# Latent attention's first eight heads: values times probabilities as three products of rounded operands in two column halves, in place of a plain fp32 product

## The chip, the cores and the metric

The kernel runs on one core of one Trainium2 chip. The metric is the device time of one execution in microseconds, median over repeated runs. Times are in us throughout.

## What is computed

The program is a stack of six layers over 512 tokens of width 1024: four mixers (convolution, forgetting attention, gated delta rule, sliding-window attention), a bidirectional linear recurrence with MLP, and multi-head latent attention with MLP. Only the latent attention changes in substance. Cut to what matters:

```python
MLA_HEADS, MLA_NOPE, MLA_ROPE, MLA_V = 16, 128, 64, 128
q = (rms_norm_2(cq, q_norm) @ w_uq).reshape(b, s, 16, 192)
k_nope, v = per head, rms_norm_2(ckv, kv_norm) @ w_ukv        # 128 + 128 columns a head
scores = (q_nope @ k_nope.T + rope(q_rope) @ rope(k_rope).T) * (128 + 64) ** -0.5
probs = softmax(scores)                                      # all 512 keys, no mask
o = probs @ v                                                # 512 x 128 a head
out = concat(o over the 16 heads) @ w_o
```

## The kernel before

**Numbers in two parts.** Nearly every product is done as three: each fp32 operand x is held as a rounded part ("high", type fp32r) and the rest ("low" = x minus high, also fp32r), and TensorE adds high times high, low times high and high times low in one PSUM bank. ScalarE makes the high part with a copy, then VectorE (or GpSimd, for the weights, line 374) the low part with a subtraction. The product of values and probabilities is an exception in this kernel: line 3339 multiplies plain fp32 tiles.

**Jobs.** Weights come as 388 jobs of 512 KB through four slots. SyncE loads them (line 284), ScalarE rounds them (line 358), GpSimd makes the low part (line 374), TensorE uses them, and each job of a slot owns one of the PSUM banks 0 to 3.

**Attention by pairs.** The sixteen heads are done as eight pairs, four in part 0 and four in part 1; each part is a loop of two trips with two pairs, followed by eight output jobs (`out_pe`). A pair begins with its projections: queries (n1 and the job's bank), keys (k0, k1) and values (v23 in an auxiliary bank, v01 in the job's bank). Then come, for head h (0 or 1) and the block of 128 queries q (0 to 3), the steps

- `s{h}{q}`: scores of 128 queries by 512 keys, five products (lines 3324 to 3328). VectorE takes the maximum (line 3505), ScalarE the exponential with its sum (line 3415) into `b.p[h][q % 2]`.
- `t{h}{q}`: VectorE divides by the sum (lines 3509 and 3510), TensorE transposes the four 128x128 blocks into a bank (line 3333), ScalarE copies them out into `b.pt[h]` (line 3419).
- `o{h}`: values times transposed probabilities into one bank (line 3339), 384 columns and then 128. ScalarE rounds the result (line 3423), VectorE makes its low part (line 3515).

**What orders the work.** The order on each engine is written out by hand: `MLA_ORDER` for TensorE, `MLA_SCALAR_ORDER` for ScalarE, `MLA_VECTOR_ORDER` for VectorE. Each engine does its list strictly in order. The steps share four auxiliary PSUM banks (4 to 7) in the ring `mla_aux`: use number u takes bank u modulo 4, and TensorE may begin a use (`ring.claim`) only when the last reader of the use four places before it has freed the bank (`ring.read`). So t02 takes the bank of s03, s13 that of s12, t12 that of t01, t03 that of t11 and o0 that of t02.

**Statistics.** The three stages `hg_post`, `ple0_post` and `mla_post` sum squares over partitions with a matmul by a matrix of ones, and `keep_busy` (line 477) fills TensorE's waits there with products whose result nobody reads: one between the sums and four behind them, 15 in all.

Of the kernel before, what the change touches and what calls it, by code (L numbers as in the profile page):

```python
# [38 lines left out]
def const_layout():  # L39

    i = np.arange(P)
    c = {}
    c["ident"] = np.eye(P)
    c["ones"] = np.ones((P, S))
    c["eps"] = np.full((P, 1), EPS)
    c["eps_squared"] = np.full((P, 1), EPS * EPS)
    c["ident2"] = np.tile(np.eye(CH), (2, 1))
    m = np.zeros((P, 2 * H8))
    for h in range(H8):
        m[[h, 32 + h], h] = 1.0  # L50
# [160 lines left out]
def hybrid_stack(nc, weights, x_t, p_t, consts, masks, params, positions, positions_2, sinks, out):  # L211
# [9 lines left out]
    with ctx:  # L221
        def sb(name, shape, dt=F32):
            return ctx.enter_context(nc.sbuf_tensor(name, shape, dt))
# [22 lines left out]
        K.w_hi = sb("weights_high", [P, SLOTS, D], F32R)  # L246
        K.w_lo = sb("weights_low", [P, SLOTS, D], F32R)
        K.X = sb("residual", [P, DT, S])
        K.M = sb("mixed", [P, DT, S])
        K.act_hi = sb("activations_high", [P, 2 * DT, S], F32R)  # L250
        K.act_lo = sb("activations_low", [P, 2 * DT, S], F32R)
        K.ident_r = sb("ident_r", [P, P], F32R)
        K.mask_r = sb("mask_r", [P, 2 * P], F32R)
        K.sel_r = sb("select_rows", [P, 2, P], F32R)
        K.sq = sb("squares", [P, 2, S])
        K.rstd, K.rstd_r = both("rstd", [P, S])
        K.root, K.root_r = both("root", [P, S])
        K.y, K.y_r = both("to_split", [P, 2, S])
        K.work = sb("work", [P, WORK])
        K.ps = [ctx.enter_context(nc.psum_tensor(f"bank{k}", [P, S], F32)) for k in range(8)]  # L260
        K.job_sems = dict(raw=[sem(f"raw_full{k}") for k in range(SLOTS)], high=sem("weights_high_ready"),
                          low=sem("weights_low_ready"), done=sem("jobs_done"),
# [131 lines left out]
def bank_of(e, c):  # L394
    return e.K.ps[c % SLOTS]
# [81 lines left out]
def keep_busy(e, n):  # L477

    K = e.K
    for _ in range(n):  # L480
        K.nc.tensor.matmul(K.ps[IDLE_BANK][:, :], K.c("ident"), K.c("ones"), start=True, stop=True)


LATE_SQUARES = 2
# [455 lines left out]
def conv_dve(e):  # L940
# [19 lines left out]
    e.eng.sem_inc(K.sem("x_ready"), DT)  # L960
    e.eng.sem_inc(K.sem("y_done"), DT)
    e.eng.wait_ge(K.sem("constants_in"), 16)
    e.steps.step(v.tensor_copy(K.ident_r[:, :], K.c("ident")))
    wf = K.param[:, K.cols["final_norm_w"]:K.cols["final_norm_w"] + DT]
    w = K.param[:, K.cols["pre_mix_norm_2"]:K.cols["pre_mix_norm_2"] + DT]
    e.steps.step(v.tensor_tensor(K.hg_cols[:, 0:DT], wf, w, ALU.mult))
# [1 line left out]
    e.steps.wait()  # L968
    e.steps.step(v.tensor_scalar(K.hg_cols[:, DT:2 * DT], K.hg_cols[:, DT:2 * DT], EPS, None, ALU.add))
    e.eng.wait_ge(K.sem("masks_in"), 16)  # L970
    v.tensor_copy(K.mask_r[:, :], K.M[:, 0, 0:2 * P]).then_inc(K.sem("masks_ready"), 1)
    e.steps.step(v.memset(b.u[:, 0:2], 0.0))
    take(renorm_vector(e, "conv", c0), 2 * DT)
    e.steps.wait()
# [201 lines left out]
def fox_dve(e):  # L1176
# [20 lines left out]
    st.wait()  # L1197
    st.step(v.tensor_tensor(x, ee, x, ALU.subtract))
    st.wait()
    st.step(v.tensor_tensor_scan(ncum, K.c("ones")[0:H8, :], x, 0.0, ALU.mult, ALU.add))  # L1200
    take(renorm, DT)
    st.wait()
    st.step(v.tensor_copy(b.rows[0:H8, :], ncum))
# [1968 lines left out]
def mla_written():  # L3172
# [12 lines left out]
MLA_SCALAR_ORDER = ["s00", "s10", "s01", "s11", "t00", "t10", "s02", "s12", "t01", "s03",  # L3185
                    "t11", "t02", "s13", "t12", "t03", "o0", "t13", "o1"]

MLA_VECTOR_ORDER = ["k0", "k1", "s00", "s10", "t00", "s01", "s11", "t10", "t01", "s02", "t11", "s12", "s03",
                    "t02", "t12", "t03", "s13", "t13", "o0", "o1"]


def mla_buffers(K):
    b = Names()
    (qr, v_tok, p, pt0, pt1) = carve(K, (DT, S), (QT, 2 * P), (2, S), (QT, S), (QT, S))
    mx, sums, rec = K.sinks[:, 0:4], K.sinks[:, 4:8], K.sinks[:, 8:12]

# [12 lines left out]
    return b
# [12 lines left out]
def mla_pe(e):  # L3222
# [50 lines left out]
    for part, out in ((0, "mla_outa"), (1, "mla_outb")):  # L3273
        c0 = FIRST_JOB[("mla_a", "mla_b")[part]]
        with e.eng.Fori(0, 2) as i:
            for s in range(2):
                trip, c = i + 2 * part, c0 + 2 * s
                mla_pair_pe(e, b, ring, ident, trip, c, i, s)
        out_pe(e, out, "mla_y", A_TILES, part * DT)
    stat_tensor(e, "mla_post")  # L3280

# [12 lines left out]
    return ins  # L3294


def mla_pair_pe(e, b, ring, ident, trip, c, i, s):

    K, nc, mm = e.K, e.K.nc, e.K.nc.tensor.matmul
    job_start(e, c, i)  # L3300
# [13 lines left out]
    for what in MLA_ORDER[4:]:  # L3314
        use, h, q = f"{what}_{s}", int(what.strip("stov")[0]), int(what[-1])
        ring.claim(use, trip)
        dst = ring.bank(use)
        if what[0] == "s":
            if q == 0:
                ring.wait_read(f"k{h}_{s}", trip)  # L3320
                ring.wait_read(f"n1_{s}", trip)
            settle(e)
            cut = slice(q * P, (q + 1) * P)
            mm(dst[:, :], b.qn_hi[:, h, cut], b.kn_hi[:, h, :], start=True, stop=False)  # L3324
            mm(dst[:, :], b.qn_lo[:, h, cut], b.kn_hi[:, h, :], start=False, stop=False)  # L3325
            mm(dst[:, :], b.qn_hi[:, h, cut], b.kn_lo[:, h, :], start=False, stop=False)
            mm(dst[:, :], b.qs[h][:, cut], b.kr_hi[:, :], start=False, stop=False)  # L3327
            ins = mm(dst[:, :], b.qs[h][:, cut], b.kr_lo, start=False, stop=True)  # L3328
        elif what[0] == "t":
            e.eng.wait_ge(K.sem(f"mla_p{h}"), trip * 8 + s * 4 + q + 1)  # L3330
            settle(e)
            for t in range(QT):
                ins = nc.tensor.transpose(dst[:, t * P:(t + 1) * P], b.p[h][q % 2][:, t * P:(t + 1) * P], ident)  # L3333
        else:
            for last, cut in ((2, slice(0, 3 * P)), (3, slice(3 * P, S))):
                ring.wait_read(f"t{h}{last}_{s}", trip)
                settle(e)
                for t in range(QT):
                    ins = mm(dst[:, cut], b.v_tok[:, t, h * P:(h + 1) * P], b.pt[h][:, t, cut],  # L3339
                             start=t == 0, stop=t == QT - 1)  # L3340
        ring.written(ins)


def mla_act(e):
# [41 lines left out]
    for part, out in ((0, "mla_outa"), (1, "mla_outb")):  # L3386
        c0 = FIRST_JOB[("mla_a", "mla_b")[part]]
        with e.eng.Fori(0, 2) as i:
            for s in range(2):
# [13 lines left out]
                weight_high(e, c + 1 + AHEAD, i)  # L3403
                use = f"v23_{s}"
                ring.wait(use, trip)
                ring.read(use, act(mla_flat(b.v_tok, 2), ring.bank(use)[:, :], ACT.Copy))
                job_wait(e, c + 1, i)
                act(mla_flat(b.v_tok, 0), bank_of(e, c + 1)[:, :], ACT.Copy).then_inc(K.job_sems["bank"][(c + 1) % SLOTS], 1)
                for what in MLA_SCALAR_ORDER:
                    use, h, q = f"{what}_{s}", int(what[1]), int(what[-1])  # L3410
                    if what[0] == "s":
                        e.eng.wait_ge(K.sem(f"mla_max{h}"), trip * 8 + s * 4 + q + 1)
# [3 lines left out]
                                           accum_out=b.stat(b.sum, h, q)))  # L3416
                    elif what[0] == "t":
                        ring.wait(use, trip)
                        ring.read(use, act(b.pt[h][:, :, q * P:(q + 1) * P],
                                           ring.bank(use)[:, :].rearrange("p (a d) -> p a d", d=P), ACT.Copy))  # L3420
                    else:
                        ring.wait(use, trip)
                        act(at(K.act_hi, i * 4 + 2 * s + h), ring.bank(use)[:, :], ACT.Copy) \
# [8 lines left out]
def mla_dve(e):  # L3432
# [43 lines left out]
    for part, out in ((0, "mla_outa"), (1, "mla_outb")):  # L3476
        c0 = FIRST_JOB[("mla_a", "mla_b")[part]]
        with e.eng.Fori(0, 2) as i:
            st.enter(i, 2 * MLA_STEPS)
            for s in range(2):  # L3480
                trip, c = i + 2 * part, c0 + 2 * s
                high = K.sem("mla_high")
# [9 lines left out]
                    e.eng.wait_ge(high, trip * 12 + s * 6 + 3 + h)  # L3492
                    step(v.tensor_tensor(b.qs[h][other, :], turned[own, :], b.qs[h][own, :].bitcast(F32), ALU.subtract))
                e.eng.sem_inc(K.sem("mla_staged"), 1)
                for what in MLA_VECTOR_ORDER:
                    use, h, q = f"{what}_{s}", int(what.strip("stovk")[0]), int(what[-1])
                    if what[0] == "k":
                        ring.wait(use, trip)
                        e.eng.wait_ge(high, trip * 12 + s * 6 + 5 + h)
                        ring.read(use, v.tensor_tensor(b.kn_lo[:, h, :], ring.bank(use)[:, :],  # L3500
# [174 lines left out]
```

## Time and profile before

| what | value |
|---|---|
| median of 3 runs | 2720.49 (2719.74 to 2721.52) |
| the profiled execution, its own time | 2723.37 |
| its span | 2721.6 |
| granted TensorE clock, mean | 0.996 |
| busy: TensorE, VectorE, ScalarE, GpSimd | 2666.7, 1394.2, 1231.0, 1076.5 |

A row of the timeline gives the start, the duration, the engine, the line of the program, the operation with its output and inputs, how many records were merged, and in brackets how long the engine had been idle and who ended that. The durations of TensorE's records overlap, since matmuls are pipelined; the distance from one start to the next is what a matmul costs in a stream. One plain fp32 matmul leaves two records. The projections and the steps of one attention pair repeat almost to the nanosecond from pair to pair.

### The profile page before, as it was taken

The page shows a single profiled execution, that of the slowest core. Times are in us where ns is not written, and L with a number is a line of the kernel's source. Part 1 is how long each engine was busy: PE and PEld are TensorE (multiplying, and loading weights), DVE is VectorE, ACT ScalarE, POOL GpSimd, SP SyncE. Part 2 cuts the span into 40 slices and gives each one's busy share as a digit, 9 for nine tenths or more (in the row PEclk, how much of TensorE's full clock was granted, in tenths as well). Part 3 has the DMA queues.
Part 4 walks back from the last instruction along what each step waited for, and adds up shares of the span by engine and source line. Part 5 has one row for each costly group of instructions (what it writes and reads, how often), then busy time and mean ns, then how long its engine had stood idle before and what let it go on. Part 6 is the DMA issues. An engine that isn't in the chain of part 4 may idle for free.

```text
span 2721.6 us, 41980 instructions
## 1 busy us (share of the span) xinstructions
PE 2666.7 (98%) x13878; PEld 2135.9 (78%) x13878; DVE 1394.2 (51%) x2452; ACT 1231.0 (45%) x1916; POOL 1076.5 (40%) x803
## 2 busy tenths in 40 slices
PE   7999999989999999999999999999999999999999
PEld 6887777767777777788887888887778887888886
DVE  7335333677778567787755321128753454221126
ACT  5324433555554455565544433235554463333234
POOL 5554333324233333443434544444412213544442
PEclk9999999999999999999999999999999999999999
DMA  4332222211121222222222333332211212333331
GB/s 159 102 99 85 77 76 71 70 55 56 37 62 47 68 70 63 85 78 67 72 70 85 101 98 95 92 112 85 78 39 46 62 31 70 101 100 92 95 106 55
DMA packets 59643, 211.89 MB, mean 78 GB/s; under 512 B 6688, under 2 KB 7072, under 8 KB 59552
## 3 DMA queue, kind: packets, MB, share of 16 engines
q1 hardware_dynamic: 57744, 206.89, 25.5%
q10 hardware_dynamic: 1520, 2.75, 0.3%
q8 instruction: 56, 0.92, 0.1%
q0 software_dynamic: 288, 1.05, 0.1%
q14 instruction: 35, 0.29, 0.0%
HBM read 208.57 MB, written 2.10 MB: 77 GB/s over the span
## 4 chain that ended last, share of the span: by engine, by line
PE 69%; DVE 5%; issue 2%; ACT 2%; POOL 0%; DVEq 0%; ACTq 0%; POOLq 0%
PE bank L1327 18%; PE bank L1329 17%; PE bank L1328 17%; PE bank L3339 2%; PE bank L1455 2%; PE bank L3333 1%; PE bank L424 1%; DVE activations_low L454 1%; PE bank L426 1%; PE bank L425 1%; PE bank L1480 1%; PE bank L3324 1%; PE bank L2191 1%; PE bank L3327 1%; PE bank L3325 1%
## 5 line engine op out<-in xcount | busy, mean ns | idle before, releaser
L374 POOL TENSOR_TENSOR weights_low<-weights_raw,weights_high 128x512 fp32r<-128x512 f32 x776 | 1047.3, 1373 | 1450.0 <-ACT weights_high L358 1425.4
L1327 PE MATMUL bank<-activations_high,weights_high 128*128 128x512 f32 x2912 | 1179.1, 405 | 29.6 <-POOL weights_low L374 13.1
L1329 PE MATMUL bank<-activations_high,weights_low 128*128 128x512 f32 x2912 | 1140.1, 392 | 0.0
L1328 PE MATMUL bank<-activations_low,weights_high 128*128 128x512 f32 x2912 | 1139.2, 391 | 0.0
L1327 PEld LDWEIGHTS bank<-activations_high,weights_high 128*128 128x128 f32 x2912 | 549.4, 189 | 164.5 <-issue 18.6
L1329 PEld LDWEIGHTS bank<-activations_high,weights_low 128*128 128x128 f32 x2912 | 548.7, 188 | 116.4
L1328 PEld LDWEIGHTS bank<-activations_low,weights_high 128*128 128x128 f32 x2912 | 550.0, 189 | 108.6 <-issue 6.7
L358 ACT ACTIVATE weights_high<-weights_raw 128x1024 fp32r<-128x1024 f32 x384 | 404.0, 1053 | 282.1 <-PE bank L1329 275.2
L2972 DVE TENSOR_TENSOR mixed<-bank,mixed 128x512 f32 (+1 forms) x48 | 33.2, 692 | 193.9 <-PE bank L1329 193.9
L2916 ACT ACTIVATE to_split<-work 128x512 f32<-128x512 f32 x64 | 40.5, 632 | 181.5 <-DVE work L2958 181.5
L2958 DVE SCALAR_TENSOR_TENSOR work<-bank,rstd 128x512 f32<-128x512 f32 x64 | 44.2, 690 | 140.2 <-PE bank L1329 134.1
L2963 DVE TENSOR_TENSOR activations_low<-to_split,activations_high 128x512 f32 x64 | 46.6, 728 | 104.6 <-ACT activations_high L2918 104.6
L1455 PEld LDWEIGHTS bank<-work 64*64 64x64 f32 x1344 | 47.4, 134 | 30.5 <-issue 30.5
L1036 ACT ACTIVATE activations_high<-to_split 128x512 fp32r<-128x512 f32 (+1 forms) x24 | 15.2, 632 | 103.3 <-DVE to_split L2370 48.1
L3505 DVE TENSOR_REDUCE sink_rows<-bank 128x1 f32<-128x512 f32 x64 | 44.1, 689 | 30.0 <-PE bank L3328 28.7
L1455 PE MATMUL bank<-work 64*64 64x64 f32 x1344 | 58.3, 223 | 1.0 <-DVE work L1966 0.9
L3339 PE MATMUL bank<-work 128*128 128x384 f32 (+1 forms) x256 | 58.8, 383 | 0.0
L1775 POOL TENSOR_TENSOR mixed<-mixed 128x512 f32<-128x512 f32 x7 | 9.6, 1376 | 120.6 <-ACT mixed L1694 120.6
L424 PE MATMUL bank<-activations_high,weights_high 128*128 128x512 f32 x136 | 56.5, 416 | 0.2 <-DVE activations_low L454 0.2
L1842 DVE SCALAR_TENSOR_TENSOR work<-work 128x512 f32<-128x512 f32 x66 | 54.6, 827 | 2.0 <-DVE mixed L1981 0.2
L792 DVE TENSOR_TENSOR root<-root,squares 128x512 f32<-128x512 f32 x44 | 40.1, 912 | 29.9 <-ACT squares L783 29.4
L783 ACT ACTIVATE squares<-residual 128x512 f32<-128x512 f32 x32 | 20.2, 632 | 76.9 <-DVEq L808 76.9
(473 smaller groups left out, 3334.7 us busy)
## 6 DMA issues: line engine op xcount, KB each, us to landing
weights_raw<-weights SPq DMA_DIRECT2D x388, 512.0 KB, 3.6
out_t<-residual SPq DMA_DIRECT2D x8, 256.0 KB, 2.1
residual<-x_t ACTq DMA_DIRECT2D x2, 512.0 KB, 7.5
residual<-x_t POOLq DMA_DIRECT2D x2, 512.0 KB, 9.9
work<-p_t ACTq DMA_DIRECT2D x2, 512.0 KB, 4.6
const<-consts SPq DMA_DIRECT2D x1, 713.0 KB, 12.7
const<-consts SPq DMA_DIRECT2D x1, 321.0 KB, 11.6
root<-positions ACTq DMA_DIRECT2D x1, 256.0 KB, 3.1
```

Of the source, the lines that this page charges most:

```text
L358: e.K.nc.scalar.activation(e.K.w_hi[:, s, :], e.K.raw[:, s, :], ACT.Copy).then_inc(js["high"], 1)
L374: K.nc.gpsimd.tensor_tensor(K.w_lo[:, s, part], K.raw[:, s, part], K.w_hi[:, s, part].bitcast(F32), ALU.subtract).then_inc(K.job_sems["low ...
L424: K.nc.tensor.matmul(dst, wh, K.act_hi[:, t, :], start=first, stop=False)
L1327: K.nc.tensor.matmul(dst, wh, K.act_hi[:, t, :], start=k == 0, stop=False)
L1328: K.nc.tensor.matmul(dst, wh, K.act_lo[:, t, :], start=False, stop=False)
L1329: ins = K.nc.tensor.matmul(dst, wl, K.act_hi[:, t, :], start=False, stop=k == len(tiles) - 1)
L1455: ins = mm(chunk(bank(use)[h, :], c), lhs[h, c, :], rhs[h, c, :], start=True, stop=True)
L1842: ins = v.scalar_tensor_tensor(t, u[:, n:n + S], b.taps[:, 4 * part + n:4 * part + n + 1], t, ALU.mult, ALU.add)
L2958: v.scalar_tensor_tensor(relu, bank_of(e, c0 + r)[:, :], 0.0, K.rstd[:, :], ALU.max, ALU.mult) \
L2963: v.tensor_tensor(at(K.act_lo, n + DT), K.y[:, 0, :], at(K.act_hi, n + DT).bitcast(F32), ALU.subtract).then_inc(K.sem("split_done"), 1)
L3339: ins = mm(dst[:, cut], b.v_tok[:, t, h * P:(h + 1) * P], b.pt[h][:, t, cut], start=t == 0, stop=t == QT - 1)
L3505: v.tensor_reduce(mx, ring.bank(use)[:, :], AX.X, ALU.max, negate=True).then_inc(K.sem(f"mla_max{h}"), 1)
```

## The change

In part 0 (the first eight heads) the product of values and probabilities is done in three products of rounded operands, in two halves of 256 columns. For that ScalarE's copies of the values and of the transposed probabilities now write rounded tiles (`b.v_hi`, `b.pt_hi`), and VectorE subtracts them from the same PSUM banks to make `b.v_lo` (steps v0, v1 in its list) and `b.pt_lo` (steps l00 to l13). The banks of v23, v01 and of every t step are freed by VectorE's subtraction and no longer by ScalarE's copy. VectorE's list becomes `MLA_SPLIT_ORDER`; ScalarE's differs from before only in that t03 stands ahead of t12. Part 1 stays as it was.

Beside that, the constant matrix of ones shrinks from 512 to 128 columns, `ident_r` goes, and the small rounded tables share a tensor with `b.v_lo`. With it the filling matmuls of `keep_busy` have 384 columns instead of 512, and a cumulative sum in the forgetting attention (line 1200) reads its ones from a single broadcast column.

```diff
-    c["ones"] = np.ones((P, S))
+    c["ones"] = np.ones((P, P))
...
-        K.M = sb("mixed", [P, DT, S])
+        K.M, K.M_r = both("mixed", [P, DT, S])
...
-        K.ident_r = sb("ident_r", [P, P], F32R)
-        K.mask_r = sb("mask_r", [P, 2 * P], F32R)
-        K.sel_r = sb("select_rows", [P, 2, P], F32R)
+        K.rows_r = sb("rows_rounded", [P, 2 * QT, P], F32R)
+        K.mask_r = K.rows_r[:, 0:2, :].rearrange("p a b -> p (a b)")
+        K.sel_r = K.rows_r[:, 2:4, :]
...
     for _ in range(n):
-        K.nc.tensor.matmul(K.ps[IDLE_BANK][:, :], K.c("ident"), K.c("ones"), start=True, stop=True)
+        K.nc.tensor.matmul(K.ps[IDLE_BANK][:, 0:3 * P], K.c("ident"), K.const[:, 0:3 * P], start=True, stop=True)
...
-    e.steps.step(v.tensor_copy(K.ident_r[:, :], K.c("ident")))
...
-    st.step(v.tensor_tensor_scan(ncum, K.c("ones")[0:H8, :], x, 0.0, ALU.mult, ALU.add))
+    st.step(v.tensor_tensor_scan(ncum, K.c("ones")[0:H8, 0:1].broadcast_to([H8, S]), x, 0.0, ALU.mult, ALU.add))
...
+MLA_SPLIT_SCALAR = ["s00", "s10", "s01", "s11", "t00", "t10", "s02", "s12", "t01", "s03",
+                    "t11", "t02", "s13", "t03", "t12", "o0", "t13", "o1"]
+
+MLA_COPIES = [use for use in MLA_SPLIT_SCALAR if use[0] == "t"]
+
+MLA_SPLIT_ORDER = ["k0", "k1", "v0", "v1", "s00", "s10", "t00", "s01", "s11", "t10", "t01", "l00", "s02", "t11", "l10", "s12",
+                   "l01", "s03", "t02", "t12", "l11", "t03", "s13", "l02", "t13", "l03", "l12", "o0", "l13", "o1"]
...
+        elif halves:
+            own = slice(h * P, (h + 1) * P)
+            ring.wait_read(f"v23_{s}", trip)
+            evacuated(e, c + 1, i)
+            for last, cut in ((1, slice(0, 2 * P)), (3, slice(2 * P, S))):
+                ring.wait_read(f"t{h}{last}_{s}", trip)
+                settle(e)
+                for t in range(QT):
+                    mm(dst[:, cut], b.v_hi[:, t, own], b.pt_hi[h][:, t, cut], start=t == 0, stop=False)
+                    mm(dst[:, cut], b.v_hi[:, t, own], b.pt_lo[h][:, t, cut], start=False, stop=False)
+                    ins = mm(dst[:, cut], b.v_lo[:, t, own], b.pt_hi[h][:, t, cut], start=False, stop=t == QT - 1)
...
+                if part == 0:
+                    act(mla_flat(b.v_hi, 2), ring.bank(use)[:, :], ACT.Copy).then_inc(K.sem("mla_rounded"), 1)
+                    job_wait(e, c + 1, i)
+                    act(mla_flat(b.v_hi, 0), bank_of(e, c + 1)[:, :], ACT.Copy).then_inc(K.sem("mla_rounded"), 1)
...
+                        if part == 0:
+                            act(b.pt_hi[h][:, :, q * P:(q + 1) * P], src, ACT.Copy).then_inc(K.sem("mla_rounded"), 1)
...
+                    if what[0] == "v":
+                        e.eng.wait_ge(K.sem("mla_rounded"), trip * 20 + s * 10 + 1 + h)
+                        bank = bank_of(e, c + 1) if h else ring.bank(f"v23_{s}")
+                        step(v.tensor_tensor(mla_flat(b.v_lo, 2 - 2 * h), bank[:, :], mla_flat(b.v_hi, 2 - 2 * h).bitcast(F32),
+                                             ALU.subtract))
...
+                    elif what[0] == "l":
+                        use, cut = f"t{what[1:]}_{s}", slice(q * P, (q + 1) * P)
+                        e.eng.wait_ge(K.sem("mla_rounded"), trip * 20 + s * 10 + 2 + MLA_COPIES.index(f"t{what[1:]}") + 1)
+                        ring.read(use, v.tensor_tensor(b.pt_lo[h][:, :, cut], ring.bank(use)[:, :].rearrange("p (a d) -> p a d", d=P),
+                                                       b.pt_hi[h][:, :, cut].bitcast(F32), ALU.subtract))
```

On VectorE, in the middle of a pair of part 0, from the maximum of s02 to that of s03. Before (3505 is the maximum, 3509 and 3510 the division; `squares` and `work` hold the two heads' probabilities):

```order
L3505 TENSOR_REDUCE sink_rows<-bank 128x1
L3509 RECIPROCAL sink_rows<-sink_rows 128x1
L195 REGISTER_ALU
L3510 TENSOR_SCALAR squares<-squares,sink_rows 128x512
L1290 REGISTER_ALU
L3505 TENSOR_REDUCE sink_rows<-bank 128x1
L1290 REGISTER_ALU
L3505 TENSOR_REDUCE sink_rows<-bank 128x1
```

The same place after the change (3549 is the maximum, 3553 and 3554 the division, 3539 the new subtraction):

```order
L3549 TENSOR_REDUCE sink_rows<-bank 128x1
L3553 RECIPROCAL sink_rows<-sink_rows 128x1
L195 REGISTER_ALU
L3554 TENSOR_SCALAR squares<-squares,sink_rows 128x512
L3538 REGISTER_ALU
L3539 TENSOR_TENSOR mixed_rounded<-bank,work_rounded 128x4x128
L1289 REGISTER_ALU
L3549 TENSOR_REDUCE sink_rows<-bank 128x1
L3538 REGISTER_ALU
L3539 TENSOR_TENSOR mixed_rounded<-bank,work_rounded 128x4x128
L1289 REGISTER_ALU
L3549 TENSOR_REDUCE sink_rows<-bank 128x1
```

Between the maxima of s02 and s12 the subtraction l10 has come in, and between those of s12 and s03 the subtraction l01; another, l00, stands right ahead of the first row.

On TensorE, the end of a pair of part 0. Before (3333 is a transpose, 3339 the product of values and probabilities):

```order
L3333 MATMUL bank<-const,work 128x128 x4
L1283 REGISTER_ALU
L3339 MATMUL bank<-work 128x384 x4
L3339 MATMUL bank<-work 128x128 x4
L3333 MATMUL bank<-const,squares 128x128 x4
```

After the change (3344 is the transpose; the three lines 3353 to 3355 come eight times for a head, four for each half of the columns):

```order
L3344 MATMUL bank<-const,work 128x128 x4
L1282 REGISTER_ALU
L3353 MATMUL bank<-work_rounded 128x256
L3354 MATMUL bank<-mixed_rounded,work_rounded 128x256
L3355 MATMUL bank<-work_rounded,rows_rounded 128x256
```

Eight plain fp32 matmuls of a head have become 24 rounded ones of 256 columns; the transposes around them stand where they stood.

## Rows read from the trace of the kernel before

**Rows 1.** The page: the span, and busy time of each engine

```profile
span 2721.6 us, 41980 instructions
PE 2666.7 (98%) x13878; PEld 2135.9 (78%) x13878; DVE 1394.2 (51%) x2452; ACT 1231.0 (45%) x1916; POOL 1076.5 (40%) x803
```

**Rows 2.** Busy time of each engine over the second pair of part 0

```profile
1995.52:2025.27 29.75, 29.75 (x162) 24.05 (x160) 15.23 (x32) 17.98 (x36) 5.10 (x4) 1.00 0.12 36
```

**Rows 3.** Timeline, TensorE: projections of values, then the second pair's end

```profile
2002.45 0.28 PE L3291 MATMUL bank<-weights_high,activations_high 128*128 128x256 f32 x1
...
2005.20 0.28 PE L3293 MATMUL bank<-weights_low,activations_high 128*128 128x256 f32 x1
...
2016.49 0.63 PE L3333 MATMUL bank<-const,work 128*128 128x128 f32 x4
2016.95 0.60 PE L3333 MATMUL bank<-const,squares 128*128 128x128 f32 x4
2017.39 0.60 PE L3333 MATMUL bank<-const,work 128*128 128x128 f32 x4
2017.89 3.71 PE L3339 MATMUL bank<-work 128*128 128x384 f32 x16
2021.44 0.60 PE L3333 MATMUL bank<-const,squares 128*128 128x128 f32 x4
2021.88 3.64 PE L3339 MATMUL bank<-work 128*128 128x384 f32 x16
2025.27 0.47 PE L424 MATMUL bank<-activations_high,weights_high 128*128 128x512 f32 x1
```

**Rows 4.** Timeline, VectorE: two subtractions from a bank, one after the other

```profile
1973.14 1.29 DVE L3500 TENSOR_TENSOR activations_low<-bank,const_rounded 128x512 fp32r<-128x512 f32 x2 [0.33 <-DVE activations_high L3493]
```

**Rows 5.** Timeline, VectorE and ScalarE in the middle of the second pair

```profile
2011.56 0.49 DVE L3510 TENSOR_SCALAR work<-work,sink_rows 128x512 f32<-128x512 f32 x1
2011.57 1.25 ACT L3419 ACTIVATE work<-bank 128x512 f32<-128x512 f32 x2
2011.96 0.68 DVE L3505 TENSOR_REDUCE sink_rows<-bank 128x1 f32<-128x512 f32 x1
...
2012.72 0.68 ACT L3415 ACTIVATE work<-bank,sink_rows 128x512 f32<-128x512 f32 x1
...
2013.29 0.20 ACT L3415 ACTIVATION_READ_ACCUMULATOR work<-bank,sink_rows 128x1 f32 x1
2013.38 0.69 DVE L3505 TENSOR_REDUCE sink_rows<-bank 128x1 f32<-128x512 f32 x1
...
2014.11 0.69 ACT L3415 ACTIVATE squares<-bank,sink_rows 128x512 f32<-128x512 f32 x1 [0.62 <-DVE sink_rows L3505]
...
2014.55 0.69 DVE L3505 TENSOR_REDUCE sink_rows<-bank 128x1 f32<-128x512 f32 x1 [0.47 <-PE bank L3328]
...
2014.98 0.60 ACT L3419 ACTIVATE work<-bank 128x512 f32<-128x512 f32 x1
...
2015.16 0.15 DVE L3509 RECIPROCAL sink_rows<-sink_rows 128x1 f32<-128x1 f32 x1
2015.35 0.49 DVE L3510 TENSOR_SCALAR work<-work,sink_rows 128x512 f32<-128x512 f32 x1
...
2015.48 0.68 ACT L3415 ACTIVATE work<-bank,sink_rows 128x512 f32<-128x512 f32 x1
...
2015.75 0.15 DVE L3509 RECIPROCAL sink_rows<-sink_rows 128x1 f32<-128x1 f32 x1
```

**Rows 6.** Timeline, TensorE: the four last filling matmuls of mla_post

```profile
2294.37 3.60 PE L481 MATMUL bank<-const 128*128 128x512 f32 x8
```

**Rows 7.** Two waits of TensorE: first pair of part 0, and behind rows 6

```profile
1973.94 0.47 PE L3324 MATMUL bank<-const_rounded,to_split_rounded 128*128 128x512 f32 x1 [1.89 <-DVE activations_low L3500]
...
2299.02 0.50 PE L1327 MATMUL bank<-activations_high,weights_high 128*128 128x512 f32 x1 [1.06 <-DVE activations_low L2470]
```

**Rows 8.** Busy time and granted clock right behind the first of them

```profile
1974.85:1978.25 3.40, 3.40 (x10) 2.65 (x9) 1.12 (x2) 0.78 (x2) 0.00 (x0) 0.50 0.53 154
```

More of the change, by code:

```diff
@@ L258, in hybrid_stack @@
         K.y, K.y_r = both("to_split", [P, 2, S])
-        K.work = sb("work", [P, WORK])
+        K.work, K.work_r = both("work", [P, WORK])
         K.ps = [ctx.enter_context(nc.psum_tensor(f"bank{k}", [P, S], F32)) for k in range(8)]
@@ L970, in conv_dve @@
     e.eng.wait_ge(K.sem("masks_in"), 16)
-    v.tensor_copy(K.mask_r[:, :], K.M[:, 0, 0:2 * P]).then_inc(K.sem("masks_ready"), 1)
+    v.tensor_copy(K.mask_r, K.M[:, 0, 0:2 * P]).then_inc(K.sem("masks_ready"), 1)
     e.steps.step(v.memset(b.u[:, 0:2], 0.0))
@@ L3205, in mla_buffers @@
     b.v_tok, b.pt = v_tok, [pt0, pt1]
+    b.v_hi, pt0_hi, pt1_hi = (K.work_r[:, first:first + QT * n].rearrange("p (a b) -> p a b", a=QT)
+                              for first, n in ((DT * S, 2 * P), (WORK - 2 * QT * S, S), (WORK - QT * S, S)))
+    b.pt_hi, b.pt_lo = [pt0_hi, pt1_hi], [K.M_r[:, 0:QT, :], K.M_r[:, QT:2 * QT, :]]
+    b.v_lo = K.rows_r[:, :, :].rearrange("p (a h) d -> p a (h d)", a=QT)
     b.stat = lambda a, h, q: a[:, 2 * h + q % 2:2 * h + q % 2 + 1]
@@ L3277, in mla_pe @@
                 trip, c = i + 2 * part, c0 + 2 * s
-                mla_pair_pe(e, b, ring, ident, trip, c, i, s)
+                mla_pair_pe(e, b, ring, ident, trip, c, i, s, part == 0)
         out_pe(e, out, "mla_y", A_TILES, part * DT)
@@ L3294, in mla_values, with mla_pair_pe @@
     return ins
-def mla_pair_pe(e, b, ring, ident, trip, c, i, s):
+def mla_pair_pe(e, b, ring, ident, trip, c, i, s, halves):
     K, nc, mm = e.K, e.K.nc, e.K.nc.tensor.matmul
@@ L3405, in mla_act @@
                 ring.wait(use, trip)
[L3406 to L3409, printed above, removed]
+                if part == 0:
+                    act(mla_flat(b.v_hi, 2), ring.bank(use)[:, :], ACT.Copy).then_inc(K.sem("mla_rounded"), 1)
+                    job_wait(e, c + 1, i)
+                    act(mla_flat(b.v_hi, 0), bank_of(e, c + 1)[:, :], ACT.Copy).then_inc(K.sem("mla_rounded"), 1)
+                else:
+                    ring.read(use, act(mla_flat(b.v_tok, 2), ring.bank(use)[:, :], ACT.Copy))
+                    job_wait(e, c + 1, i)
+                    act(mla_flat(b.v_tok, 0), bank_of(e, c + 1)[:, :], ACT.Copy).then_inc(K.job_sems["bank"][(c + 1) % SLOTS], 1)
+                for what in (MLA_SPLIT_SCALAR if part == 0 else MLA_SCALAR_ORDER):
                     use, h, q = f"{what}_{s}", int(what[1]), int(what[-1])
@@ L3418, in mla_act @@
                         ring.wait(use, trip)
-                        ring.read(use, act(b.pt[h][:, :, q * P:(q + 1) * P],
-                                           ring.bank(use)[:, :].rearrange("p (a d) -> p a d", d=P), ACT.Copy))
+                        src = ring.bank(use)[:, :].rearrange("p (a d) -> p a d", d=P)
+                        if part == 0:
+                            act(b.pt_hi[h][:, :, q * P:(q + 1) * P], src, ACT.Copy).then_inc(K.sem("mla_rounded"), 1)
+                        else:
+                            ring.read(use, act(b.pt[h][:, :, q * P:(q + 1) * P], src, ACT.Copy))
                     else:
@@ L3478, in mla_dve @@
         with e.eng.Fori(0, 2) as i:
-            st.enter(i, 2 * MLA_STEPS)
+            st.enter(i, 2 * (MLA_STEPS + (2 if part == 0 else 0)))
             for s in range(2):
@@ L3494, in mla_dve @@
                 e.eng.sem_inc(K.sem("mla_staged"), 1)
-                for what in MLA_VECTOR_ORDER:
-                    use, h, q = f"{what}_{s}", int(what.strip("stovk")[0]), int(what[-1])
-                    if what[0] == "k":
+                for what in (MLA_SPLIT_ORDER if part == 0 else MLA_VECTOR_ORDER):
+                    use, h, q = f"{what}_{s}", int(what.strip("stovkl")[0]), int(what[-1])
+                    if what[0] == "v":
[3 more added lines that the diff above has]
+                                             ALU.subtract))
+                        if h:
+                            release(e, c + 1)
+                        else:
+                            e.eng.sem_inc(ring.free[ring.find(f"v23_{s}")[1]], 1)
+                    elif what[0] == "l":
[3 more added lines that the diff above has]
+                                                       b.pt_hi[h][:, :, cut].bitcast(F32), ALU.subtract))
+                    elif what[0] == "k":
                         ring.wait(use, trip)
```

## The prediction

> **What bounds the kernel now.** I read the page first: TensorE is busy 98% of the span, VectorE and ScalarE about half [rows 1]. So what counts is which work TensorE does and where it stands still. Then the second pair of part 0 by windows: it takes 29.75 us, TensorE is busy all of it, VectorE 15.23 and ScalarE 17.98 [rows 2]. By these sums VectorE has room. But a share over a pair hides an order, so I read the timeline of that pair engine by engine [rows 3, 5]. The other pairs have the same steps at the same distances, so one pair tells for all. Below I leave out the thousands: 11.96 is 2011.96.
>
> **What TensorE gains.** The product of values and probabilities takes 3.55 for o0 (17.89 to 21.44) and 3.39 for o1 (21.88 to 25.27), 3.47 on average [rows 3]. The new one is 24 matmuls of 256 columns on rounded operands. The projection of the values has just that shape: 24 of them, the first starting at 2.45 and the last at 5.20, so 2.75 / 23 = 0.12 from start to start [rows 3]. That makes 24 x 0.12 = 2.88, with some 0.09 for the first weight load 2.97: a gain of 0.5 a head, 1.0 a pair, 4.0 for the eight heads of part 0.
>
> The Trainium skill (TensorE: Matmul & The Clock Gate, Back-to-back issue gap) gives N / 2.4 + 2.5 ns for one matmul behind another, 109 ns at 256 columns. The row shows 120, and this case's trace decides. By the page's figure a head would take 24 x 0.109 = 2.62, and the gain of part 0 would be about 6 in place of 4.
>
> **What VectorE gets.** Ten subtractions a pair from a PSUM bank: v0, v1 and eight l steps. The nearest row is the low part of the keys, also bank minus SBUF tile, 128x512: two in 1.29, so 0.69 for one and the next one 0.60 later [rows 4]. The l steps have the form 4x128 with gaps between the runs, which no row of VectorE here shows; I take 0.69, with 0.90 as upper end. That is some 6 a pair, 15.2 + 6 = 21 of 29.75. The sum fits; the order decides.
>
> **The chain through the middle of a pair.** From the rows: a maximum takes 0.69 and VectorE goes on after 0.61 (14.55, 15.16); the exponential starts 0.04 behind it (13.38 + 0.69, 14.11); its sum is there 0.77 after its start (12.72, then 13.29 + 0.20); a division takes 0.59 (15.16 to 15.75), its scaling starting 0.19 in and taking 0.49; a copy takes 0.60 [rows 5]. Before, the maxima of s02, s12, s03 start at 11.96, 13.38, 14.55 and the exponentials at 12.72, 14.11, 15.48 [rows 5]. Now in the new order:
>
> - l00 stands ahead of s02's maximum and needs the copy of t00, which starts at 11.57 and ends at 12.17. So l00 at 12.2, the maximum of s02 at 12.8 instead of 11.96.
> - Then t11's division and l10: s12's maximum at 12.8 + 0.61 + 0.59 + 0.60 = 14.6 instead of 13.38, its exponential at 15.33 instead of 14.11.
> - ScalarE has t01's copy behind that exponential: 16.0 to 16.6. VectorE has nothing it may do before l01, since s03's maximum stands behind it. So it idles from 15.2 to 16.65; then l01, and s03's maximum at 17.25 instead of 14.55, its exponential at 17.98, done at 18.75.
> - t02 takes the bank of s03. It started 0.24 after that exponential was done (16.25, 16.49) and now starts at 18.99: 2.5 late. s13, which takes the bank of s12, waits before it until 16.2, but that wait lies inside the same delay.
> - VectorE goes on with two divisions, then l11 (copy of t11 done at 19.26), then t03's division from 19.9, scaled at 20.58: t03 at 20.64 instead of 17.39, 3.25 late.
> - o0 takes the bank of t02, now free only after l02, and l02 stands behind s13's maximum (20.49): 21.10 to 21.79. o0 at 21.85 instead of 17.89, 3.96 late.
> - o0 takes 2.97 instead of 3.55 and ends 3.38 late, at 24.82; l03 is done just when its second half needs it.
> - o1's first half follows t13, its second half needs l13, which stands behind the copies of o0 and t13 (to 26.24) and o0's low part: done at 27.1, where the first half is through at 26.79. A wait of 0.36. The pair ends at 28.59 instead of 25.27.
>
> So a pair costs 3.3 more although its matmuls cost 1.0 less: TensorE stands still for about 1.0 ahead of s13, 1.5 ahead of t02, 0.75 ahead of t03, 0.75 ahead of o0, 0.4 in o1. Four pairs: 13.2. In the first pair, where TensorE starts the scores late behind the keys anyway [rows 7], I take the same: v0 and v1 need copies that are long done. Nothing behind the pair hides it, since the next job starts when o1 ends.
>
> **The rest.** v0 and v1 go before s00's maximum; TensorE has two more banks for scores then, and they shift it by 0.2, which is made up for by s01. The weights' jobs are three ahead and GpSimd is busy 5.1 of 29.75 [rows 2], so ScalarE's later copies cost them nothing. The smaller table at the start, the dropped copy of `ident_r` and the broadcast ones are one instruction or a part of a transfer each that TensorE doesn't wait for: 0, at most 0.5 either way.
>
> A filling matmul of 512 columns takes about 0.86 (3.60 less a tail of 0.2, for four [rows 6]); with 384 it is 0.21 less. The one between the sums is on the path in three stages: 0.6 gained. The four behind them cover the wait for the next stage, which then starts 1.06 after them [rows 7] and now 1.06 + 0.85 = 1.9.
>
> **The clock.** Once TensorE waited 1.89 [rows 7], and right after it the granted clock was 0.5 for 3.4 us, the level of 1.2 GHz, with 10 matmuls in that time [rows 8]. Full work in such a stretch loses half of it, 1.7. The wait of 1.9 behind the filling is as long; whether the clock falls I can't tell from one row, so of three places I count 1.2, that is 2.0. In a pair the waits sum to 4 within 6.6 us; I expect the clock to fall in most pairs, but part of the 3.4 us is waiting anyway, so 0.9 a pair, 3.5. The bounds of both: 0, and 7 x 1.7 = 11.9.
>
> **Sum.** 13.2 - 0.6 + 2.0 + 3.5 = 18.1. The profiled execution: span 2721.6 [rows 1], own time 2723.37, so 2741.5 for it; the median of the runs is 2.9 lower than its own time, so 2738.6, which I round to 2738. Without any fall of the clock 2733, with all of them 2745.
>
> **The rivals.**
>
> - *VectorE's subtractions stay hidden, faster.* For it speaks that VectorE is busy for only half of a pair [rows 2]. Then TensorE's gain stands alone: 4.0 + 0.6, that is 2716. It decides itself at the maximum of s03: t02 had 0.24 between the end of that exponential and its own start, of which little is slack, and the products give back 1.0 a pair. So the maximum must come no more than about 1.2 late; I have it 2.7 late. It takes subtractions of under 0.3, and rows 4 have 0.69. Chance 0.10.
> - *Half of the delay*, because engines go on sooner than I add up: 1 to 1.5 a pair, 2722 to 2726. Chance 0.07.
> - *Longer subtractions.* At 0.90 for the 4x128 form, five of them on the chain add 1.0 a pair, with the clock 2745 to 2750. Against it: the scaling and the copies of this pair read or write at the usual rate. Chance 0.07.
> - *The forecast*, 2728 to 2745, with its clock terms open. Chance 0.76.
>
> **How the numbers follow.** A measurement of this kernel tells about 0.2% (5.4 us) from no change. Slower by more than that: the forecast and the longer subtractions, 0.83. Within it: half of the delay, 0.07. Faster, 2716 being 4.6 below the median, just within 0.2%, goes partly there: of the 0.10 I give 0.05 to each side. The range 2725 to 2746 leaves out the first rival and most of the second below, and the tail of the third above.
>
> **What would show it.** In the second pair after the change: its length 33 us and not 29; o0's stretch 2.97 with rounded tiles; maxima of s02, s12, s03 late by 0.8, 1.2, 2.7 against the scores' start; VectorE idle ahead of l01, released by ScalarE's copy; t02, t03, o0 released by ScalarE and VectorE after waits. Clock at 0.5 in several pairs and behind the filling matmuls. Part 1 unchanged. I am wrong if t02 follows s13 without a wait, or if a subtraction takes far from 0.69.

## The result, and the profile after

The changed kernel takes 2741.16 us (median of 6 runs, 2737.78 to 2741.89) against 2721.01 for the kernel before: ratio 1.0071, 95% interval 1.006 to 1.0082. It is 20 us slower, where 17.5 were forecast. Its profiled execution has a span of 2738.9, its own time is 2740.74.

The page of the changed kernel, its span and busy times, to be read beside [rows 1]:

```profile
span 2738.9 us, 42211 instructions
PE 2664.8 (97%) x13942; PEld 2143.3 (78%) x13942; DVE 1421.4 (52%) x2491; ACT 1231.2 (45%) x1916; POOL 1076.2 (39%) x803
```

TensorE has 1.9 less to do in a span that is 17.3 longer, so it stands still for longer. VectorE has 27 more, which are the 40 subtractions of 0.69 less the dropped copy of `ident_r`. The percentages hardly tell the two kernels apart.

The second and the third pair of part 0 after the change, windows (length, busy time of TensorE, weight loads, VectorE, ScalarE, GpSimd, then the granted clock), beside [rows 2]:

```profile
1999.97:2034.41 34.44, 30.92 (x177) 26.18 (x176) 21.68 (x42) 18.17 (x36) 5.08 (x4) 0.95 0.11 32
2034.41:2068.00 33.59, 29.61 (x177) 25.00 (x176) 21.68 (x42) 18.29 (x36) 5.09 (x4) 1.00 0.11 31
```

A pair took 29.75 and now takes 33.6 to 34.4, and TensorE is idle for 3.5 to 4.0 of that, VectorE still for 12 to 13. From the first score to the next job the eight pairs took 19.95 each before, but for the first one with 21.58. After the change the four of part 0 take 26.60, 24.74, 23.89 and 24.83, those of part 1 still 19.95. That is 18.6 more in part 0. The third pair is the one whose clock stayed up, so I read the steps there.

VectorE in the third pair, the middle, to be read beside [rows 5] (3549 is the maximum, 3539 the new subtraction):

```profile
2050.97 0.69 DVE L3539 TENSOR_TENSOR mixed_rounded<-bank,work_rounded 128x512 fp32r<-128x512 f32 x1
2051.58 0.68 DVE L3549 TENSOR_REDUCE sink_rows<-bank 128x1 f32<-128x512 f32 x1
...
2052.77 0.68 DVE L3539 TENSOR_TENSOR mixed_rounded<-bank,work_rounded 128x512 fp32r<-128x512 f32 x1
2053.37 0.68 DVE L3549 TENSOR_REDUCE sink_rows<-bank 128x1 f32<-128x512 f32 x1
2055.38 0.69 DVE L3539 TENSOR_TENSOR mixed_rounded<-bank,work_rounded 128x512 fp32r<-128x512 f32 x1 [1.33 <-ACT work_rounded L3448]
2055.99 0.68 DVE L3549 TENSOR_REDUCE sink_rows<-bank 128x1 f32<-128x512 f32 x1
...
2064.73 0.69 DVE L3559 TENSOR_TENSOR activations_low<-bank,activations_high 128x512 f32 x1 [2.11 <-ACT activations_high L3453]
2065.64 0.69 DVE L3539 TENSOR_TENSOR mixed_rounded<-bank,work_rounded 128x512 fp32r<-128x512 f32 x1 [0.22 <-DVE activations_low L3559]
```

The fifth row is l01. VectorE idles 1.33 ahead of it, released by ScalarE's copy of t01, with the maximum of s03 standing ready behind it. The scores of this pair start at 2044.11, those of the second pair before at 2005.32. Against these starts the maxima of s02, s12 and s03 are 0.83, 1.20 and 2.65 later than before.

TensorE in the same pair, beside [rows 3] (3335 begins a score, 3344 is a transpose, 3353 the first of the three products):

```profile
2055.01 0.47 PE L3335 MATMUL bank<-const_rounded,to_split_rounded 128*128 128x512 f32 x1 [0.63 <-ACT squares L3442]
...
2057.72 0.63 PE L3344 MATMUL bank<-const,work 128*128 128x128 f32 x4 [1.32 <-ACT work L3442]
...
2059.44 0.63 PE L3344 MATMUL bank<-const,work 128*128 128x128 f32 x4 [0.65 <-DVE work L3554]
2060.64 0.36 PE L3353 MATMUL bank<-work_rounded 128*128 128x256 f32 x1 [0.57 <-DVE mixed_rounded L3539]
...
2063.67 0.60 PE L3344 MATMUL bank<-const,squares 128*128 128x128 f32 x4
2064.02 0.36 PE L3353 MATMUL bank<-work_rounded 128*128 128x256 f32 x1
...
2066.48 0.36 PE L3353 MATMUL bank<-work_rounded 128*128 128x256 f32 x1 [0.79 <-DVE mixed_rounded L3539]
...
2067.99 0.40 PE L424 MATMUL bank<-activations_high,weights_high 128*128 128x512 f32 x1
```

The waits stand ahead of s13, t02, t03, o0 and the second half of o1. Their releasers are ScalarE's exponentials of s12 and s03, VectorE's scaling for t03, and VectorE's subtractions l02 and l13. o0 takes 3.03 (2060.64 to 2063.67), and o1 3.97 with its wait inside.

The granted clock in four stretches, in the order of the rows: in the second pair, behind the filling of `hg_post`, in the fourth pair, and at the first pair's start (as before, [rows 8]). All four are at 0.5. Behind the two other fillings the clock stays at 1.0; the first pair has a second such stretch at 1990.74.

```profile
2024.87:2028.28 3.41, 3.16 (x14) 2.82 (x15) 3.03 (x6) 1.75 (x4) 0.00 (x0) 0.50 0.00 0
...
1482.15:1485.57 3.42, 3.42 (x8) 2.74 (x9) 3.42 (x7) 1.84 (x3) 0.00 (x0) 0.50 0.00 0
2093.14:2096.55 3.41, 3.22 (x15) 2.85 (x15) 2.78 (x6) 1.75 (x4) 0.00 (x0) 0.50 0.00 0
1973.67:1977.08 3.41, 3.41 (x9) 2.65 (x8) 2.17 (x4) 0.73 (x2) 0.00 (x0) 0.50 0.53 154
```

### The profile page after: what moved, and what is told of

It is laid out like the page before. It is cut to its first block, busy times and chain, and to the rows that moved or that the text cites. A ratio compares the mean times of both kernels' runs of the same rounds, so it can differ in the third digit from the quotient of the medians.

```text
span 2738.9 us, 42211 instructions
## 1 busy us (share of the span) xinstructions
PE 2664.8 (97%) x13942; PEld 2143.3 (78%) x13942; DVE 1421.4 (52%) x2491; ACT 1231.2 (45%) x1916; POOL 1076.2 (39%) x803
## 4 chain that ended last, share of the span: by engine, by line
PE 67%; DVE 6%; issue 3%; ACT 2%; POOL 0%; DVEq 0%; ACTq 0%; POOLq 0%
PE bank L1326 17%; PE bank L1328 17%; PE bank L1327 17%; PE bank L1454 2%; PE bank L3361 1%; PE bank L424 1%; DVE activations_low L454 1%; PE bank L425 1%; PE bank L426 1%; PE bank L1479 1%; PE bank L2190 1%; PE bank L3344 1%; DVE residual L2479 1%; PE bank L2203 0%; PE bank L2223 0%
## 5 line engine op out<-in xcount | busy, mean ns | idle before, releaser
L1702 ACT ACTIVATE work<-bank 128x256 f32<-128x256 f32 x40 | 15.4, 386 | 86.4 <-PE bank L1454 86.4
```

## The experiments

The pair times below run from the first score of a pair to the next job. The kernel before has 19.95, the change 23.89 where the clock stays up.

### e1: without the low part of the probabilities

```diff
-                    mm(dst[:, cut], b.v_hi[:, t, own], b.pt_lo[h][:, t, cut], start=False, stop=False)
+                    mm(dst[:, cut], b.v_hi[:, t, own], b.pt_hi[h][:, t, cut], start=False, stop=False)
...
-                            act(b.pt_hi[h][:, :, q * P:(q + 1) * P], src, ACT.Copy).then_inc(K.sem("mla_rounded"), 1)
+                            ring.read(use, act(b.pt_hi[h][:, :, q * P:(q + 1) * P], src, ACT.Copy))
...
-MLA_SPLIT_ORDER = ["k0", "k1", "v0", "v1", "s00", "s10", "t00", "s01", "s11", "t10", "t01", "l00", "s02", "t11", "l10", "s12",
-                   "l01", "s03", "t02", "t12", "l11", "t03", "s13", "l02", "t13", "l03", "l12", "o0", "l13", "o1"]
+MLA_SPLIT_ORDER = ["k0", "k1", "v0", "v1", "s00", "s10", "t00", "s01", "s11", "t10", "t01", "s02", "t11", "s12",
+                   "s03", "t02", "t12", "t03", "s13", "t13", "o0", "o1"]
...
-                        e.eng.wait_ge(K.sem("mla_rounded"), trip * 20 + s * 10 + 1 + h)
+                        e.eng.wait_ge(K.sem("mla_rounded"), trip * 4 + s * 2 + 1 + h)
```

> The eight subtractions of a pair that make the low part of the transposed probabilities are left out, and their banks are freed by ScalarE's copy again; the product takes the high part twice, so TensorE's 24 matmuls a head stay (the output lacks the low part's share). Theory, that the order of VectorE's subtractions holds TensorE up: the waits ahead of s13, t02, t03 and o0 go, and a pair of part 0, from its first score to the next job, takes 18.9 to 19.3 (19.95 before the change, 23.89 with it), the whole about 2716 to 2719. Rival, that the rounded products or v0 and v1 cost the time: a pair stays above 22.

(The sum has high times high twice, so its output is wrong by more than the low part, and it tells of the times alone.) A pair takes 18.83, a little less than expected, and the whole 2719.28 in a single run, beside 2721.0 for the kernel before. That is just above the expected range; the clock fell in this run at the first pair's start (20.47 for that pair) and behind two of the three fillings. TensorE's timeline of its third pair, where o0 begins, the transpose behind it and where o1 begins:

```profile
2044.63 0.36 PE L3353 MATMUL bank<-work_rounded 128*128 128x256 f32 x1
...
2047.58 0.60 PE L3344 MATMUL bank<-const,squares 128*128 128x128 f32 x4
2047.94 0.36 PE L3353 MATMUL bank<-work_rounded 128*128 128x256 f32 x1
```

2.95 a head, and no wait ahead of any step of that pair. So the rounded products gain 1.1 a pair (1.04 in o0 and o1, 0.08 in the transposes between them), v0 and v1 cost nothing, since o0 starts 12.57 after the first score as before, and all of the loss sits in the eight l steps, with the banks that they free: 23.89 - 18.83 = 5.1 a pair.

### e2: the subtractions without the new products

```diff
-            for last, cut in ((1, slice(0, 2 * P)), (3, slice(2 * P, S))):
+            for last, cut in ((2, slice(0, 3 * P)), (3, slice(3 * P, S))):
                 ring.wait_read(f"t{h}{last}_{s}", trip)
                 settle(e)
                 for t in range(QT):
-                    mm(dst[:, cut], b.v_hi[:, t, own], b.pt_hi[h][:, t, cut], start=t == 0, stop=False)
-                    mm(dst[:, cut], b.v_hi[:, t, own], b.pt_lo[h][:, t, cut], start=False, stop=False)
-                    ins = mm(dst[:, cut], b.v_lo[:, t, own], b.pt_hi[h][:, t, cut], start=False, stop=t == QT - 1)
+                    ins = mm(dst[:, cut], b.v_hi[:, t, own].bitcast(F32), b.pt_hi[h][:, t, cut].bitcast(F32),
+                             start=t == 0, stop=t == QT - 1)
```

> All ten subtractions of a pair stay, in the same order, but the product is again eight plain fp32 matmuls a head in 384 and 128 columns, on the high parts alone (the low parts are made and not used, so the output lacks them). Theory: o0 starts 4.0 late as with the change, and nothing is given back by faster products, but o1's wait for its last subtraction is hidden by the longer first part; a pair takes 23.7 to 24.2 undisturbed by the clock. Rival, that the time goes into the rounded products: a pair near 21 or below.

The pairs take 28.61, 24.01, 24.15 and 24.24, the whole 2744.65. Only in the second did the clock stay up; it fell in the third and fourth, and in the first at its start and again for 6.8. In the second pair o0 starts 16.64 after the first score, with the change 16.53, before 12.57. The delay of 4 is there with the old products too. From o0 to the next job e2 takes 7.37 and the change 7.35: nearly all that the new products gain in time goes, with the change, into o1's wait for l13.

### e3: one exchange

```diff
-                   "l01", "s03", "t02", "t12", "l11", "t03", "s13", "l02", "t13", "l03", "l12", "o0", "l13", "o1"]
+                   "s03", "l01", "t02", "t12", "l11", "t03", "s13", "l02", "t13", "l03", "l12", "o0", "l13", "o1"]
```

> One exchange in VectorE's list: the maximum of s03 ahead of the subtraction l01. Theory: s03's maximum no longer waits for ScalarE's copy of t01 and comes about 1.2 late instead of 2.7; t02 waits about 0.9 less, and a pair takes 23.0 in place of 23.89; the waits ahead of s13 (1.0), t03 (0.8) and o0 (1.0) stay. Rival, that VectorE simply has too much to do in this stretch: 23.7 to 23.9, since its work is the same.

The second to fourth pair take 23.05 each, as worked out, with the same instructions. The first, in which the clock fell at the start, takes 24.69, and the whole 2737.76. t02 starts 12.71 after the first score instead of 13.62. The rival, too much work for VectorE, is out by this run: the work was the same.

### e4: new orders on VectorE and ScalarE

```diff
-MLA_SPLIT_SCALAR = ["s00", "s10", "s01", "s11", "t00", "t10", "s02", "s12", "t01", "s03",
-                    "t11", "t02", "s13", "t03", "t12", "o0", "t13", "o1"]
+MLA_SPLIT_SCALAR = ['s00', 's10', 's01', 't00', 's11', 't10', 's02', 's12', 't01', 't11', 's03', 't02', 's13', 't03', 't12', 't13', 'o0', 'o1']
...
+MLA_SPLIT_ORDER = ['k0', 'k1', 'v0', 'v1', 's00', 's10', 't00', 's01', 't10', 's11', 't01', 'l00', 's02', 'l10', 't11', 's12', 't02', 's03', 't12', 'l01', 'l11', 's13', 't03', 'l02', 'l03', 't13', 'l12', 'l13', 'o0', 'o1']
```

> The same instructions as with the change, in other orders on VectorE and ScalarE (TensorE's order stays): maxima and divisions first, subtractions l01, l11, l02, l03 where VectorE would otherwise wait, and ScalarE's exponentials ahead of its copies. Theory, worked out with the durations of the trace: a pair takes 20.6 (19.95 before, 23.89 with the change), with waits of about 0.4 ahead of s13 and t02 and 0.7 ahead of t03, and the clock stays up in most pairs. Rival, that ten more subtractions can't be hidden in any order: above 22.

20.97 a pair in the second to fourth, 0.4 more than expected, the clock at 1.0 in all four, the whole 2727.73. Three quarters of the pair's loss (2.92 of 3.94) were in the order. What is left are idle times of TensorE of 0.2 ahead of s13, 0.3 ahead of t02 and 0.6 ahead of t03, which I put down to its own order (e6 changes that too): t02 starts at 12.10, t03 at 13.72 and o0 at 14.32 after the first score (before 11.16, 12.06, 12.57).

### e5: the shorter filling alone, in the kernel before

```diff
-        K.nc.tensor.matmul(K.ps[IDLE_BANK][:, :], K.c("ident"), K.c("ones"), start=True, stop=True)
+        K.nc.tensor.matmul(K.ps[IDLE_BANK][:, 0:3 * P], K.c("ident"), K.const[:, 0:3 * P], start=True, stop=True)
```

> The kernel before with one edit of the change alone: the filling matmuls behind the sums of squares have 384 columns instead of 512. Theory: the wait behind the four of them grows by 0.85 to about 1.9 at three places, the granted clock falls to 0.5 for 3.4 us behind one or two of them, 1.7 us each, and 0.2 us a place is gained between the sums; the whole 1 to 3 us slower. Rival, that the filling only fills: 0.6 us faster, and no fall of the clock near 1483, 1899 and 2299.

2723.14 (11 runs) against 2721.95, ratio 1.0005 with an interval of 0.9996 to 1.0014: in time alone inconclusive. The profile shows the mechanism at two of the three places. The wait behind the third filling, and windows right behind the second, the third and the first filling:

```profile
2293.40 2.75 PE L481 MATMUL bank<-const 128*128 128x384 f32 x8
...
2298.05 0.50 PE L1327 MATMUL bank<-activations_high,weights_high 128*128 128x512 f32 x1 [1.91 <-DVE activations_low L2470]
```

```profile
1899.80:1903.20 3.40, 3.40 (x9) 2.66 (x9) 3.40 (x6) 2.08 (x4) 0.00 (x0) 0.50 0.00 0
2299.20:2302.60 3.40, 3.40 (x10) 2.63 (x9) 3.40 (x6) 1.92 (x4) 0.00 (x0) 0.50 0.00 0
1483.73:1487.13 3.40, 3.40 (x15) 2.82 (x16) 3.40 (x7) 1.80 (x3) 0.00 (x0) 1.00 0.00 0
```

The wait is 1.91 as reckoned. Behind the second and the third filling TensorE did 9 and 10 matmuls in 3.4 us at a clock of 0.5, and behind the first 15 at a clock of 1.0. In e3, the change with 384 columns as well, the clock fell behind all three:

```profile
1483.64:1487.05 3.41, 3.41 (x10) 2.63 (x9) 3.41 (x7) 1.53 (x3) 0.00 (x0) 0.50 0.00 0
1900.07:1903.48 3.41, 3.41 (x10) 2.63 (x9) 3.41 (x6) 1.94 (x4) 0.00 (x0) 0.50 0.00 0
2313.08:2316.49 3.41, 3.41 (x9) 2.65 (x8) 3.41 (x6) 1.85 (x4) 0.00 (x0) 0.50 0.00 0
```

Over the six traces with 384 columns (the change 1, e1 2, e2 2, e3 3, e4 2, e5 2) it fell behind 12 of 18 fillings. In the four with 512 or 464 columns (the kernel before, e6, e7, e8) it fell behind none of 12.

### e6 and e7: new orders on all three engines

Besides new lists as in e4, TensorE gets a list of its own for part 0, in which the two halves of a product are steps, with a list of banks to match, and the filling has 464 columns. The lists of e6:

```diff
+MLA_SPLIT_SCALAR = ['s00', 's10', 's01', 't00', 's02', 't10', 't01', 's11', 's03', 't02', 's12', 't03', 's13', 't11', 't12', 't13', 'o0', 'o1']
+MLA_SPLIT_ORDER = ['k0', 'k1', 'v0', 's00', 'v1', 's10', 't00', 's01', 't10', 's02', 't01', 'l00', 't02', 'l10', 's11', 's03', 'l01', 's12', 't11', 't03', 'l02', 's13', 't12', 'l03', 't13', 'l11', 'l12', 'l13', 'o0', 'o1']
+MLA_SPLIT_PE = ['s00', 's10', 's01', 's02', 't00', 't10', 's11', 't01', 's03', 's12', 't02', 's13', 't11', 't03', 'o0a', 't12', 'o0b', 't13', 'o1a', 'o1b']
...
-    for what in MLA_ORDER[4:]:
+    for what in (MLA_SPLIT_PE if halves else MLA_ORDER[4:]):
...
-            for last, cut in ((1, slice(0, 2 * P)), (3, slice(2 * P, S))):
+            for last, cut in (((1, slice(0, 2 * P)), (3, slice(2 * P, S)))[half],):
...
-        K.nc.tensor.matmul(K.ps[IDLE_BANK][:, 0:3 * P], K.c("ident"), K.const[:, 0:3 * P], start=True, stop=True)
+        K.nc.tensor.matmul(K.ps[IDLE_BANK][:, 0:464], K.c("ident"), K.const[:, 0:464], start=True, stop=True)
```

> The change with new orders on VectorE, ScalarE and also TensorE in part 0 (the two halves of a product may stand apart, with a transpose between them), and 464 columns in the filling matmuls instead of 384. Theory, worked out with the trace's durations: all ten subtractions hidden, waits of 0.4 ahead of t10 and 0.1 at a few places, a pair of part 0 in 19.4 to 19.7 (19.95 before, 23.89 with the change, 20.97 with two new orders), the clock not down behind the filling; the whole 2718 to 2720, 1 to 3 us faster than before. Rival, that subtractions which free banks cost TensorE waits in any order: a pair above 20.5, 2723 or more.

> As the run before it, with other lists for the three engines, chosen for shorter waits of TensorE where the durations come out a little longer than reckoned. Theory: a pair in 19.5 to 19.8, the whole 2718 to 2721.

e6 takes 2719.01 (11 runs) against 2721.95 (27 runs of the kernel before on the same chip), ratio 0.9989, interval 0.998 to 0.9998; e7 2719.59, ratio 0.9992, interval 0.9982 to 1.0001, so that e7 alone is not shown to be faster. The second to fourth pairs take 19.74 in e6 and 19.67 in e7, just above and inside what was expected. Windows of e6, a pair of part 0 and behind the first filling:

```profile
2021.67:2051.00 29.33, 29.05 (x176) 24.96 (x174) 21.09 (x42) 18.12 (x36) 5.08 (x4) 1.00 0.13 36
1482.46:1485.86 3.40, 3.40 (x15) 2.83 (x16) 3.40 (x7) 1.80 (x3) 0.00 (x0) 1.00 0.00 0
```

VectorE is as busy as with the change, 21 in a pair, and TensorE stands still for 0.3 instead of 4. The idea of the change is then worth something, if little: from one pair's first score to the next 29.43 in e6 and 29.37 in e7, instead of 29.75. Over four pairs that is 1.3 and 1.5. The rest of e6's 2.9 lies elsewhere, some 0.7 of it ahead of the first filling (see the sum below). New orders alone could hardly give as much to the kernel before, whose TensorE has no idle time in a pair [rows 2]; no run tries it.

### e8: the change with a longer filling

The edit is the last one of e6 alone, in the changed kernel.

> The change with the filling matmuls at 464 columns instead of 384, all else the same. Theory: the waits behind the filling are 1.06 + 0.32 = 1.4 and the clock stays up there; the pairs stay as with the change (23.9 and 24.8 by the clock); the whole 1 to 3 us faster than the change, 2738 to 2740. Rival: within 0.5 us of the change's 2741.2, and the clock falls there as well.

2738.32 (4 runs, ratio to before 1.0063, interval 1.0048 to 1.0079), where the change had 1.0071; the intervals overlap, so the gain of some 2 us is not shown by the times. The clock is, behind all three fillings:

```profile
1480.60:1484.00 3.40, 3.31 (x14) 2.73 (x15) 3.40 (x7) 1.71 (x3) 0.00 (x0) 1.00 0.00 0
1895.90:1899.30 3.40, 3.37 (x15) 2.79 (x16) 3.40 (x7) 1.77 (x3) 0.00 (x0) 1.00 0.00 0
2311.20:2314.60 3.40, 3.33 (x15) 2.75 (x16) 3.40 (x7) 1.73 (x3) 0.00 (x0) 1.00 0.00 0
```

The pairs take 24.93, 23.90, 24.85 and 23.90: the clock fell in two of them.

## Why the prediction was right

**The chain.** All its steps are in the third pair, and the delays against the start of the scores are the forecast ones, but for the last:

| step | forecast late | measured late |
|---|---|---|
| maximum of s03 | 2.7 | 2.65 |
| t02 | 2.5 | 2.45 |
| t03 | 3.25 | 3.27 |
| o0 | 3.96 | 3.96 |
| t13 | 3.38 | 3.44 |
| the next job | 3.32 | 3.94 |

It was argued from the rows of the kernel before, and is shown by e1 (without the l steps it is gone), e2 (it stays without the new products) and e3 (one exchange moves it by the amount worked out).

**What was mis-sized in it.** The wait inside o1: forecast 0.36, and the second half came about 0.9 late. From o0's end to the end of l13 I had 2.28 (24.82 to 27.1), and it took 2.66 (2063.67 to 2066.33). In that stand 0.22 of idle time that the row of l13 shows: in this program the step of o0's low part waits for its own end before VectorE goes on. Between the end of l13 (2066.33) and TensorE's start (2066.48) lie 0.15, where the forecast has 0.05, and the first half of o1 was through 0.1 sooner behind o0's end than forecast. So the pair was 0.6 dearer than forecast, 2.5 in all. By e1 the products' gain was 1.1 a pair and not 1.0; a head took 2.95 there, with 2.97 forecast.

**The form of the l steps.** The open price of 4x128 subtractions was 0.69, the lower end, so the rival of longer subtractions is out. Half of the delay, 1 to 1.5 a pair, is out by the 3.94. The first rival is out by the result, and e1 shows what it would have been worth, 1.1 a pair; e6 shows that some 0.3 of that can be had, from one first score to the next, by other orders on three engines.

**The clock in the pairs.** Forecast 0.9 in each. It fell in the first, second and fourth, which are 5.02, 4.79 and 4.88 longer than before against 3.94 in the third: 0.85 to 1.1 for a fall, 2.9 in all instead of 3.5.

**The filling.** Forecast +2.0 - 0.6. In the profiled execution the wait behind the four became 1.99 at `hg_post` and 1.91 and 1.92 at the two others, and the clock fell behind the first alone. By how far the same work before and behind a filling is shifted between the two traces, that place cost 1.3 (some 1.5 for the fall, less 0.2 for the shorter filling), and the two others gained 0.2 each: 0.9 for the three. e5 puts all three places at about 1.2 us in time, within its uncertainty of the forecast 1.4. That the clock falls because of the filling's length is shown by the traces together: 12 of 18 times with 384 columns, 0 of 12 with 464 or 512, and in e8, where the length is the only edit, 0 of 3.

**The sum.** Forecast 17.5 against the earlier median. In the trace, the span is 17.3 longer. Of that 18.2 lie between the first score of part 0 and the first of part 1 (the pairs themselves add 18.6, the work around them gives 0.4 back), and 0.9 in the three fillings. Ahead of the first filling the changed kernel is 1.7 shorter, where the forecast has 0, at most 0.5. About 0.7 of this lies between 635 and 871, in the gated delta rule, and recurs in all eight traces with the change and in neither of the two without it (the kernel before and e5); what makes it is not shown. The other 1.0 arises before 573, where the clock is down at other places: near 541 and 562 before, near 42 and 564 after (the stretch near 906 is shorter after, 3.4 instead of 6.8, and moves nothing). That part differs between traces of the changed kernels too (e2 and e7 have the stretch near 541, e3, e6 and e8 one between 39 and 43), so it is chance.

So the closeness of the sum is in part luck. The pairs were 1.9 dearer than forecast (2.5 by the mis-sized wait, less 0.6 of the clock), and that was more than made up for by 0.5 in the fillings, 0.4 around the pairs and the 1.7 ahead of them. By the medians the change costs 20.15, some 2.7 more than forecast. 2.8 of them stand in the medians and not in the spans of these two traces, which can't show where they lie.

## What to carry to other kernels

Where engines work through lists in strict order, price an added instruction by the place it gets and not by its engine's spare time: with the same ten subtractions and the same new products a pair became 3.9 longer, 1.0 longer or 0.2 shorter by order alone, and what another engine waits for belongs ahead of what only frees a bank late. When a step that frees a shared buffer moves from one engine to another, go through every later claim of that buffer. And filling work that seems free may be what keeps the clock up: here a quarter less of it let the clock fall 12 times of 18.

## What was not expected of the hardware

The length of a wait alone doesn't decide whether the clock falls. Behind 1.91 to 1.99 us of waiting it fell at one place of three with the change and at two others in e5, and in the kernel before a pair start with a wait of 1.89 let it fall [rows 7, 8] where the same place in e5 did not: there the first pair took 20.02 instead of 21.58. That wait is 1.88 to 1.89 in all ten traces, and the clock fell behind it in five (before, the change, e1, e2, e3) and not in the five others. What decides it no run here shows.
